# Feed-forward gate and up products of a two-block network: one 512-column product for the high weights, and a PSUM bank for each half

## What is computed

```python
STAGES = ("ffn", "even", "ffn", "ffn", "mla", "ffn", "ffn", "fox", "ffn")
x = x + 0.5 * (silu(rmsnorm(x) @ w_gate) * (rmsnorm(x) @ w_up)) @ w_down   # d_ff = 2816
```

## Time and profile before

| what | value |
|---|---|
| median of 3 runs (lowest to highest) | 1580.22 us (1578.76 to 1582.55) |
| the profiled execution | 1580.43 us |
| its span | 1578.6 us |
| mean granted TensorE clock | 0.992 |
| instructions | 29272 |
| busy: PE, weight loads, DVE, ACT, POOL | 97%, 90%, 50%, 48%, 33% of the span |
| DMA | 259.93 MB, mean 165 GB/s |

### The profile page before, as it was taken

The page is one execution under the profiler, slowest core; times in us unless marked ns, Lnnn a source line. Parts: engine busy times, 40 slices in busy tenths (PEclk is TensorE's granted clock), DMA queues, the critical chain, the costliest instruction groups (busy, mean ns, idle before and its releaser), DMA issues.

```text
span 1578.6 us, 29272 instructions
## 1 busy us (share of the span) xinstructions
PE 1534.0 (97%) x11720; PEld 1415.1 (90%) x11720; DVE 788.6 (50%) x1053; ACT 765.6 (48%) x1053; POOL 513.5 (33%) x201
## 2 busy tenths in 40 slices
PE   7999999999999999999999999999999999999997
PEld 7999988897999998999987999999999887899996
DVE  4443456457534444444565543445444588754443
ACT  5444365234643454434576544345434577554433
POOL 2444400000344336344352344434344300044342
PEclk9999999999999999999999999999999999999999
DMA  6554431133454544545452455454545462345442
GB/s 254 198 199 181 178 134 68 56 109 136 183 187 174 198 160 161 199 170 189 163 174 103 160 198 186 174 199 162 200 170 189 163 211 81 107 164 195 184 176 92
DMA packets 48086, 259.93 MB, mean 165 GB/s; under 512 B 5376, under 2 KB 5632, under 8 KB 27296
## 3 DMA queue, kind: packets, MB, share of 16 engines
q1 hardware_dynamic: 47664, 258.68, 44.4%
q10 hardware_dynamic: 288, 0.34, 0.1%
q0 software_dynamic: 80, 0.14, 0.0%
HBM read 258.08 MB, written 1.05 MB: 164 GB/s over the span
## 4 chain that ended last, share of the span: by engine, by line
PE 89%; ACT 4%; DVE 3%; POOL 2%; issue 1%; DMA 1%; SPq 0%; DVEq 0%; POOLq 0%; ACTq 0%
PE banks L367 81%; PE banks L1257 1%; ACT gu_hi L338 1%; DVE x L474 1%; DVE gu_lo L347 1%; DMA raw_gu<-units_gu 1%; PE banks L1264 1%; ACT arena L402 1%; ACT h_hi L385 0%; PE banks L2652 0%; PE banks L1234 0%; POOL dn_lo L360 0%; DVE arena L2380 0%; PE banks L2048 0%; ACT arena L2262 0%
## 5 line engine op out<-in xcount | busy, mean ns | idle before, releaser
L360 POOL TENSOR_TENSOR dn_lo<-raw_dn,dn_hi 128x1024 fp32r<-128x1024 f32 x138 | 478.1, 3465 | 891.3 <-ACT dn_hi L343 883.7
L367 PE MATMUL banks<-h_hi,gu_hi 128*128 128x256 f32 x2256 | 644.0, 285 | 10.3 <-DVE h_lo L418 5.8
L367 PE MATMUL banks<-h_lo,gu_hi 128*128 128x256 f32 x2256 | 640.3, 284 | 0.0
L367 PE MATMUL banks<-h_hi,gu_lo 128*128 128x256 f32 x2256 | 640.2, 284 | 0.0
L347 DVE TENSOR_TENSOR gu_lo<-raw_gu,gu_hi 128x2048 fp32r<-128x2048 f32 x161 | 370.0, 2298 | 216.4 <-ACT gu_hi L338 216.4
L367 PEld LDWEIGHTS banks<-h_hi,gu_hi 128*128 128x128 f32 x2256 | 434.2, 192 | 17.7 <-issue 5.1
L367 PEld LDWEIGHTS banks<-h_lo,gu_hi 128*128 128x128 f32 x2256 | 434.3, 193 | 6.0 <-issue 1.3
L367 PEld LDWEIGHTS banks<-h_hi,gu_lo 128*128 128x128 f32 x2256 | 434.3, 192 | 0.0
L338 ACT CAST gu_hi<-raw_gu 128x2048 fp32r<-128x2048 f32 x161 | 306.5, 1904 | 39.4 <-DMA raw_gu<-units_gu 24.1
L482 ACT ACTIVATE silu<-silu 128x256 f32<-128x256 f32 x132 | 55.2, 418 | 520.6 <-DVE silu L490 520.5
L367 PE MATMUL banks<-dn_hi,act_hi 128*128 128x512 f32 x528 | 207.9, 394 | 3.4 <-POOL dn_lo L360 3.4
(11 more groups left out here) (336 smaller groups left out, 1309.6 us busy)
## 6 DMA issues: line engine op xcount, KB each, us to landing
raw_gu<-units_gu SPq DMA_DIRECT2D x161, 1024.0 KB, 6.0
raw_dn<-units_dn SPq DMA_DIRECT2D x162, 512.0 KB, 3.5
x<-x_in SPq DMA_DIRECT2D x2, 512.0 KB, 5.2
raw_gu<-units_gu SPq DMA_DIRECT2D x2, 512.0 KB, 7.7
out<-x SPq DMA_DIRECT2D x1, 1024.0 KB, 3.9
cst<-constants SPq DMA_DIRECT2D x1, 688.0 KB, 12.1
lora<-low_rank SPq DMA_DIRECT2D x1, 512.0 KB, 12.9
arena<-final_gain SPq DMA_DIRECT2D x1, 512.0 KB, 4.1
```

What stands on the lines that cost most here:

```text
L360: nc.gpsimd.tensor_tensor(dn_lo[:, p, 0:n], raw_dn[:, p, 0:n], dn_hi[:, p, 0:n].bitcast(F32), ALU.subtract).then_inc(dn_lo_ready, 1)
L367: ins = nc.tensor.matmul(out, a, b, start=first and i == 0, stop=last and i == 2)
```

## The change

`h_hi` and `h_lo` become two halves of one tile, so that for each block k the high and the low part lie side by side, 512 columns. For each side and block, one matmul of 512 columns multiplies the high weights by both, and one of 256 columns adds the low weights by the high input. Columns 0 to 255 of a bank then hold high by high plus low by high, and columns 256 to 511 high by low. The gate half has bank 2p and the up half bank 2p+1, each with a signal of its own (`gate_summed`, `gu_used`). ACT copies columns 256 to 511 of each bank to `lo_half` in SBUF, DVE adds them to columns 0 to 255; the gate's sum is then multiplied by the row of inverse roots, SBUF by SBUF, and the last product is `silu` by `act32`, SBUF by SBUF as well. The row of inverse roots goes through bank 7. The two mixer routines that write `h_hi` and `h_lo` write them through the new layout.

```diff
@@ -264,7 +264,8 @@
         gu_hi, gu_lo = sb("gu_hi", [P, 2, GU], F32R), sb("gu_lo", [P, 2, GU], F32R)
         dn_hi, dn_lo = sb("dn_hi", [P, 2, DN], F32R), sb("dn_lo", [P, 2, DN], F32R)
         x = sb("x", [P, 2, D])
-        h_hi, h_lo = sb("h_hi", [P, KD, T], F32R), sb("h_lo", [P, KD, T], F32R)
+        h_both = sb("h_both", [P, KD, 2, T], F32R)
+        h_hi, h_lo = h_both[:, :, 0, :], h_both[:, :, 1, :]
         silu = sb("silu", [P, 2, T])
         act32 = sb("act32", [P, 2, T])
         act_hi, act_lo = sb("act_hi", [P, 2, T], F32R), sb("act_lo", [P, 2, T], F32R)
@@ -310,7 +311,8 @@
         gu_hi_ready, gu_lo_ready = sem("gu_hi_ready"), sem("gu_lo_ready")
         dn_hi_ready, dn_lo_ready = sem("dn_hi_ready"), sem("dn_lo_ready")
         gu_used, dn_used = sem("gu_used"), sem("dn_used")
-        gate_ready = sem("gate_ready")
+        gate_ready, gate_summed, lo_copied, halves_added = (sem(n) for n in ("gate_ready", "gate_summed", "lo_copied",
+                                                                             "halves_added"))
         silu_ready, act_ready = sem("silu_ready"), sem("act_ready")
         act_hi_ready, act_lo_ready = sem("act_hi_ready"), sem("act_lo_ready")
         squares_ready, rstd_ready = sem("squares_ready"), sem("rstd_ready")
@@ -323,6 +325,8 @@
         first_gate_landed, first_gate = sem("first_gate_landed"), sem("first_gate")
         GATE_HALF, UP_HALF = slice(0, D), slice(D, 2 * D)
 
+        lo_half = arena[:, 16, 0:4 * T].rearrange("p (u i t) -> p u i t", u=2, i=2)
 
         def landed(eng, sems, pair, p):
             eng.wait_ge(sems[p], 16 * (pair + 1))
@@ -445,12 +449,12 @@
 
             pe.wait_ge(diag_ready, ffn_index(s) + 1)
             for t in range(2):
-                ins = nc.tensor.matmul(banks[:, 2, t * P:(t + 1) * P], const("ones"), rstd_diag[:, t, :], start=True, stop=True)
+                ins = nc.tensor.matmul(banks[:, 7, t * P:(t + 1) * P], const("ones"), rstd_diag[:, t, :], start=True, stop=True)
             ins.then_inc(row_summed, 1)
 
         def rstd_row_act(act, s):
             act.wait_ge(row_summed, ffn_index(s) + 1)
-            nc.scalar.copy(rstd_row, banks[:, 2, 0:T]).then_inc(row_ready, 1)
+            nc.scalar.copy(rstd_row, banks[:, 7, 0:T]).then_inc(row_ready, 1)
 
         def ffn_index(s):
             return sum(k == "ffn" for k in stages[:s])
@@ -478,19 +482,28 @@
 
         def ffn_act(act, pair, p, f, ahead):
             hi_dn(act, pair, p)
+            act.wait_ge(gate_summed, f + 1)
+            nc.scalar.copy(lo_half[:, p, 0, :], banks[:, 2 * p, T:2 * T]).then_inc(lo_copied, 1)
             act.wait_ge(gate_ready, f + 1)
             nc.scalar.activation(silu[:, p, :], silu[:, p, :], ACT.Silu).then_inc(silu_ready, 1)
+            act.wait_ge(gu_used, 2 * pair + p + 1)
+            nc.scalar.copy(lo_half[:, p, 1, :], banks[:, 2 * p + 1, T:2 * T]).then_inc(lo_copied, 1)
             act.wait_ge(act_ready, f + 1)
             nc.scalar.copy(act_hi[:, p, :], act32[:, p, :]).then_inc(act_hi_ready, 1)
             if ahead:
                 hi_gu(act, pair + 1, p)
 
         def ffn_dve(dve, pair, p, f, ahead):
-            dve.wait_ge(gu_used, 2 * pair + p + 1)
-            nc.vector.tensor_tensor(silu[:, p, :], banks[:, p, 0:T], rstd_row, ALU.mult).then_inc(gate_ready, 1)
+            dve.wait_ge(lo_copied, 2 * f + 1)
+            nc.vector.tensor_tensor(silu[:, p, :], banks[:, 2 * p, 0:T], lo_half[:, p, 0, :], ALU.add).then_inc(halves_added, 1)
+            dve.wait_ge(halves_added, 2 * f + 1)
+            nc.vector.tensor_tensor(silu[:, p, :], silu[:, p, :], rstd_row, ALU.mult).then_inc(gate_ready, 1)
+            dve.wait_ge(lo_copied, 2 * f + 2)
+            nc.vector.tensor_tensor(act32[:, p, :], banks[:, 2 * p + 1, 0:T], lo_half[:, p, 1, :],
+                                    ALU.add).then_inc(halves_added, 1)
             dve.wait_ge(silu_ready, f + 1)
-            nc.vector.tensor_tensor(act32[:, p, :], silu[:, p, :], banks[:, p, T:2 * T],
-                                    ALU.mult).then_inc(act_ready, 1)
+            dve.wait_ge(halves_added, 2 * f + 2)
+            nc.vector.tensor_tensor(act32[:, p, :], silu[:, p, :], act32[:, p, :], ALU.mult).then_inc(act_ready, 1)
             dve.wait_ge(act_hi_ready, f + 1)
             nc.vector.tensor_tensor(act_lo[:, p, :], act32[:, p, :], act_hi[:, p, :].bitcast(F32),
                                     ALU.subtract).then_inc(act_lo_ready, 1)
@@ -510,10 +523,11 @@
                     if norm is not None and side == 0 and k % 2 == 0:
                         pe.wait_ge(h_lo_ready, 4 * norm + k // 2 + 1)
                     w = slice((side * KD + k) * P, (side * KD + k + 1) * P)
-                    ins = three_products(banks[:, p, side * T:(side + 1) * T],
-                                         (gu_hi[:, p, w], gu_lo[:, p, w]), (h_hi[:, k, :], h_lo[:, k, :]),
-                                         k == 0, k == KD - 1)
-            ins.then_inc(gu_used, 1)
+                    nc.tensor.matmul(banks[:, 2 * p + side, :], gu_hi[:, p, w],
+                                     h_both[:, k, :, :].rearrange("p i t -> p (i t)"), start=k == 0, stop=False)
+                    ins = nc.tensor.matmul(banks[:, 2 * p + side, 0:T], gu_lo[:, p, w], h_hi[:, k, :], start=False,
+                                           stop=k == KD - 1)
+                ins.then_inc((gate_summed, gu_used)[side], 1)
 
         def ffn_down(pe, pair, p, f, first, last):
             pe.wait_ge(dn_lo_ready, 2 * pair + p + 1)
@@ -1743,7 +1757,7 @@
             def outputs(g, i):
                 wait(act, MS, "pe", ("o", g, i))
                 k = 4 * g + 2 * i
-                done(cp(h_hi[:, k:k + 2, :].rearrange("p h t -> p (h t)"), banks[:, k, :]), ("hi", g, i))
+                done(cp(h_hi[:, k:k + 2, :], banks[:, k, :].rearrange("p (h t) -> p h t", h=2)), ("hi", g, i))
 
             for t in range(2):
                 square_k(0, t)
@@ -1895,8 +1909,8 @@
             def outputs(g, i):
                 wait(dve, MS, "act", ("hi", g, i))
                 k = 4 * g + 2 * i
-                done(tt(h_lo[:, k:k + 2, :].rearrange("p h t -> p (h t)"), banks[:, k, :],
-                        h_hi[:, k:k + 2, :].rearrange("p h t -> p (h t)").bitcast(F32), ALU.subtract), ("lo", g, i))
+                done(tt(h_lo[:, k:k + 2, :], banks[:, k, :].rearrange("p (h t) -> p h t", h=2),
+                        h_hi[:, k:k + 2, :].bitcast(F32), ALU.subtract), ("lo", g, i))
 
             sum_k(0, 0)
             sum_k(0, 1)
```

## The result

| kernel | median us | lowest to highest | against before, 95% interval |
|---|---|---|---|
| before | 1579.49 | 1578.41 to 1582.55 | |
| changed | 1658.69 | 1657.60 to 1659.62 | 1.0499 (1.0483 to 1.0515) |

The changed kernel is 79.2 us slower, where 75 were forecast. The table's runs of before were made beside the changed kernel's; later runs of the same kernel lie between 1576.4 and 1582.1 us.

What follows compares the result with a forecast made beforehand. TensorE's issue of matmuls was taken as the bound before, the ring of DVE, POOL and ACT after the change. 1580.4 + 65.6 for the stages + 9.5 for the clock = 1655.5, said as 1655; range 1625 to 1680.

Steps and rivals of the forecast that it cites:

- the hold: Gate product behind `gu_lo`: shut out by POOL's `dn_lo` subtraction, ending 0.28 us after it, near 2.1 us in duration.
- extrapolation from `act_lo`: Gate product with fp32 output: assumed held as `act_lo` is, 2.27 + 0.28 us, the nearest row in shape and inputs.
- The ring: DVE, POOL and ACT steps from one `gu_hi` to the next: 8.77 us a unit, longer than PE's 8.31.
- the first rival: Gate product behind `gu_lo` not held: ring 7.0 us, PE's 8.31 stays the bound, 1560 us; chance 0.12.
- One stage: A stage's steps timed from the row's copy: +12.4 us a stage, in four stages; two stages differ.
- up(2) starts at: Start of a stage: 10.36 us after the row's copy instead of 8.45, +1.9 us.
- up(21) starts: Last up of a stage: reached after nineteen periods of 8.77 instead of 8.50 us, +5.1 us.
- down(21) starts late by: End of a stage: down(21) waits 5.6 us for `act_lo`; less the shorter up, +5.4 us.
- clock behind that wait: After the longer wait at each of five stage ends: about 1.9 us lost to the lower clock, 9.5 in all.
- the last stage: Stage with no W or L (`gu_hi`, `gu_lo`) behind unit 20: its last chain comes sooner, +9.4 us.
- the stage ahead of MLA: There POOL's first `dn_lo` subtraction runs before `gu_lo`, so up(3) comes 3.6 us earlier; stage +6.6 us.
- PE's gain: Up products on TensorE: 0.348 instead of 0.360 us a pair, -0.19 a unit, -25 us over 132 units if PE alone sets the pace.

Runs made afterwards that it cites:

- e1: The changed kernel with the gate's sum written back to PSUM, so the gate product reads one input from PSUM: 1564.07 us, ratio 0.9898 to the kernel before.
- e5: The changed kernel with POOL's subtraction cut to 8 of 1024 columns, the others filled with zeros: 1562.49 us, ratio 0.9891 to the kernel before.
- e4: The changed kernel with POOL's down-weight subtraction as two instructions of 512 columns instead of one of 1024: 1566.96 us, ratio 0.9920 to the kernel before.
- e8: The kernel before with its gate product SBUF by SBUF, after an ACT copy of the gate half from PSUM: 1583.57 us, ratio 1.0021.
- e3: The changed kernel with three products of 256 columns again and the gate's sum in PSUM: 1578.56 us, ratio 0.9993 to the kernel before.
- e9: Narrow product ahead of the wide in blocks 1 to 7, against the changed kernel with both sums in PSUM and gate copy ahead of `dn_hi`: 1551.78 us.
- e6: The changed kernel with the gate's sum in PSUM for units 20 and 21 of each stage alone: 1633.74 us, ratio 1.0340 to the kernel before.

## Why the prediction was right, and where its terms were off

**The bound and the hold.** As forecast, the gate product from two SBUF inputs comes right behind `gu_lo`, when POOL's waiting subtraction has begun, and ends 0.29 us behind it (forecast 0.28), after 2.165 us. Taking one input away from SBUF (e1) or taking POOL's reads away (e5) removes the hold: 0.42 us in every unit. Halving POOL's instruction (e4) shortens it: 0.95 us in the median, 1.07 at most. In the kernel before (e8) the same product is held while POOL's subtraction is under way, and not when it has ended. What was an extrapolation from `act_lo`, that an fp32 output is held like an fp32r one, is measured. The rule on two SBUF inputs (the Trainium skill, SBUF — State Buffer, Who interferes with whom) agrees with each of these numbers. Its clause that an instruction of GpSimd that only writes SBUF does not contend agrees with e5, where the product took 0.42 us beside the fill.

**The ring.** 8.77 forecast, 8.81 measured; the addition-to-product step was 0.53 (1048.08 to 1048.61), not 0.46. Without the hold it is 7.11 (e1), where the first rival had 7.0. PE waited for `gu_lo` in front of the ups, as forecast.

**One stage, from the row's copy** (1126.35 in the changed kernel):

| step | forecast | measured |
|---|---|---|
| up(2) starts at; in the kernel before | 10.36; 8.45 | 10.48 (1136.83); 8.30 |
| up(21) starts | 177.0 | 177.6 (1303.99), 19 x 8.80 |
| down(21) starts late by | 5.6 | 5.5 (1317.95, where 1309.75 + 2.74 was possible) |
| stage against before, clock apart | +12.4 | +13.3 |
| clock behind that wait | +1.9 | +2.2 (twelve products in 4.95) |
| with the clock | +14.3 | +15.5 (196.83 against 181.36, from up(1) to the transposes behind down(21)) |

The prediction's 8.45 for up(2) in the kernel before is off: it starts at 1082.49, 8.30 behind the row's copy. That, the longer ring (0.6 by up(21)), the up of 5.75 us that saved nothing at the stage's end (0.2) and the clock (0.3) are about the missing 1.2 us.

By the same reading the six stages lost 14.5, 14.7, 9.4, 15.8, 15.5 and 12.0 us, 81.9 together, and what lies between them, mixers and edges, came out 3 us shorter; the spans differ by 78.8. The clock was near its forecast at the five ends where it was counted: the twelve products took 1.8, 2.1, 2.1, 2.5 and 2.2 us more than 2.74, 10.6 together against 9.5. It was missed in the last stage, which had a late down(21) as well (2.4 us idle before it) and seven products at half clock behind that: 1.6 us, the larger part of what made it 12.0 instead of 9.4. In the stage ahead of MLA, POOL's first subtraction did run ahead of `gu_lo`, and up(3) started 18.66 us after the row's copy against 22.04 before, 3.4 earlier (forecast 3.6); it lost 9.4 us (195.95 against 186.57), forecast 8.5 with the clock.

**PE's gain** was the term off by most, without weight here: 0.11 to 0.12 a unit, not 0.19 (e1 against e3). I had added the pitches of two unmixed sequences. The PE-bound kernel (e1) came to 1564, not to the first rival's 1560. The 0.348 a pair is not out of reach, though: 43 ups of the changed kernel run at 0.347 (see e9).

**The sum.** 75.1 us forecast as difference, 78.8 in the spans (79.2 in the medians). By stage: the four ordinary ones 4 x 14.3 = 57.2 forecast and 60.5 measured, the last 9.4 and 12.0, the one ahead of MLA 8.5 and 9.4. That is 6.8 us too little. The 3.1 us by which mixers and edges came out shorter, where nothing was forecast, go the other way; no run here explains them. So the mechanism and the ring's length were right; that the total came within 4 us and not 7 is luck.

## What to carry to other kernels

When an element-wise step is moved or its operand changes from PSUM to SBUF, ask which VectorE instructions then read two SBUF operands, and what GpSimd is doing at that moment; a sum written back to PSUM, or GpSimd's instruction cut in two, took 92 to 95 us off here without a matmul being touched. Such a hold need not cost anything lasting: in e8 the ring with it was shorter than TensorE's unit, and the whole price was 3 us. Sum the ring of in-order engines from start-to-start distances before counting what a faster TensorE saves: with 50% and 67% of busy time, ACT and DVE set the pace of a kernel in which TensorE shows 94%. And a lag that a ring builds up is paid once more where a stage drains. A clock fall can follow the wait: it did at all six ends of the changed kernel, and behind e6's 2 us waits at three of five.

## What the runs showed that was not expected

A wide product of 512 columns followed by one of 256 takes 0.3525 us on average in e1, where separate sequences take 0.228 and 0.120. Two paces lie behind it: an up runs its pairs at 0.347 or at 0.352 to 0.354, in the same order of instructions (the first up of a stage at 0.365). Most ups of the changed kernel and nearly all of e1's have the slower one. Putting the narrow product first brought 7.5 us (e9), all of it in the up half of a unit. No run here explains the two paces, or why only the up half gained.

The same wait does not always bring the same clock. Behind a wait of 1.9 to 2.0 us at the same place of a stage (e6), twelve products ran at full clock in two stages, and in three others seven or eight of them at half. What decided it in one stage and not in the next is open.
